# RWKV chunk recurrence in one transformer kernel: the second head pair's turns and first inverse products in the TensorE array's other two quarters

## The chip, the cores and the metric

The kernel runs on one core of a Trainium2 chip. The metric is the device time of one execution, in microseconds (us), the median of several runs.

## The reference

Two small blocks of two layers each, batch 1, 256 tokens, width 1024, all in fp32. The first block has a short convolution mixer, an MLP, an RWKV-7 mixer and an MLP; the second has a top-k sparse attention, an MLP, a forgetting attention and an MLP. The change lies in the RWKV-7 mixer, whose core is this recurrence for each of 16 heads of size 64 (`_wkv7_scan`, shortened):

```python
def frame_step(state, inp):                 # r, w, k, v, a, b of one token
    sa = einsum('bhvk,bhk->bhv', state, a_t)
    state = state * w_t + sa[..., None] * b_t + v_t[..., None] * k_t
    y_t = einsum('bhvk,bhk->bhv', state, r_t)
```

Here a = -kk (the normed key) and b = kk * ah. The result is normed by head, gets a bonus term, is gated and goes through `w_o`.

## The kernel before

The recurrence is computed in chunks of 64 tokens, four chunks. Within a chunk the token-by-token feedback through `sa` becomes a unit triangular 64x64 matrix that has to be inverted. The 16 heads are 8 pairs: in a pair, head 0 lies on partitions 0 to 63 and head 1 on 64 to 127 (`HEAD`). A *slot* is two pairs (`q` or `m` = 0, 1), so there are four slots, and a fifth round for what trails behind.

TensorE works on a pair by `by_head` (line 2562): one 64x64 product for each head, with the operands and the output on the same partitions. Head 0 uses the quarter of the array with rows 0 to 63 and columns 0 to 63, head 1 the quarter with rows and columns 64 to 127. The other two quarters, rows of one head and columns of the other, are not used.

`wkv_steps(slot)` gives the order of steps, and every engine walks through the same list. For slot s they are:

- `gram`, for each pair: the gram products of b and of k with a and r (64x128, into `acc[q]` and `acc[2+q]`), and between them the turn of v from feature-major to token-major (a product with a centred identity, into the second half of bank `un[q]`). VectorE makes from `acc[q]` the first inverse `inv_t`, the masked `nb_t` and the turned inverse `inv_x` (lines 1938 to 1942); ScalarE copies v to `v_tok` (1249).
- `tok`, for each pair: the turns of b and k into `un[q]`; ScalarE copies them to `bk_tok` (1252), and after the second pair makes the exponentials `w_cum`, `w_inv` of the next slot (1124, 1125). VectorE masks `nk_t` (1946).
- five levels j, each doubling the size of the inverted blocks: `t1` for each pair, `n_m` times `inv_x` into `acc[q]`, copied by ScalarE to the tile `t1` (1257); `dx` for each pair, `t1` times `inv_t` into `acc[2+q]`; VectorE adds it to `inv_t` (1951) and turns the result to `inv_x` (1954). `n_m` is masked by POOL (806).
- between these, the *chain* of the slot before, `rhs`, `u` and `sy` for each of four chunks: right-hand side, solution, and state and y. ScalarE copies `wkv_rhs` (1260) and `wkv_u` (1263), VectorE keeps and updates `state` (1963, 1969, 1971) and copies y (1929).

The order in slots 1 to 3, with the pair in brackets: gram(0), rhs, gram(1), u, tok(0), sy, tok(1); then level 1 as t1(0), rhs, t1(1), dx(0), u, dx(1); level 2 as t1(0), sy, t1(1), dx(0), rhs, dx(1); level 3 with u and sy, level 4 with rhs and u, level 5 with sy behind t1(0) alone. In slot 0 there is no chain; there `beside_steps` lays the last value products of the mixer (`value_rows`, full-array products) between the steps. In slots 1 and 2 ScalarE and VectorE also split one half of a weight tile after step 1 and after step 14 (`w_hi`, line 869, and `w_lo`, line 1460). In slots 2 and 3 there are statistics products of the group norm (2538, 2547) and a chain of three VectorE scale instructions before level 4's dx (1919, 1921, 1924). Each engine runs its own instructions in order and waits on semaphores; a step that is late holds all behind it on that engine.

Of the kernel before, what the change touches and what calls it, by code (L numbers as in the profile page):

```python
# [8 lines left out]
ACT = mybir.ActivationFunctionType  # L9
# [14 lines left out]
SLOTS = PAIRS // 2  # L24
CHUNK = 64
CHUNKS = SEQ // CHUNK
# [74 lines left out]
def build(nc, A, out):  # L101

    with ExitStack() as ctx:
        sems = {}

        def sem(name):
            if name not in sems:
                sems[name] = ctx.enter_context(nc.semaphore(name))
            return sems[name]
# [61 lines left out]
        eye, eye_centered = c_("eye"), c_("eye_centered")  # L171
# [35 lines left out]
        rw_r, rw_k, rw_v, rw_c, rw_a, rw_kk = RW  # L207
# [40 lines left out]
        v_tok, inv_t, bk_tok = [], [], []  # L248
# [356 lines left out]
        def half_bank(b, at_):  # L605
            return flat(b)[:, 2 * P * at_:2 * P * (at_ + 1)].rearrange("p (c q) -> p c q", c=CHUNKS)
# [11 lines left out]
        def _(sp):  # L618
# [82 lines left out]
        g_done, gk_done, tok_done, tok_out, inv_ready, lak_ready, end_ready = (  # L701
            sem(n) for n in ("g_done", "gk_done", "tok_done", "tok_out", "inv_ready", "lak_ready", "end_ready"))
# [16 lines left out]
        def _(pool):  # L719
# [25 lines left out]
            def build_bk(s):  # L745
                pool.wait_ge(sem("rw_ready"), s + 1)
                pool.wait_ge(sem("exp_ready"), 2 * s + 2)
                pool.wait_ge(tok_done, 2 * s)
                t = slice(2 * s, 2 * s + 2)
                G.tensor_tensor(b_fm[:].rearrange("p q c s -> p (q c s)"), rw_a[:, t, :].rearrange("p q s -> p (q s)"),  # L750
                                w_inv[:].rearrange("p q s -> p (q s)"), ALU.mult)
                G.tensor_tensor(k_fm[:].rearrange("p q c s -> p (q c s)"), rw_k[:, t, :].rearrange("p q s -> p (q s)"),
                                w_inv[:].rearrange("p q s -> p (q s)"), ALU.mult)
# [99 lines left out]
        def _(act):  # L853
# [390 lines left out]
            for slot in range(SLOTS + 1):  # L1244
                for n, (step, s, j, q) in enumerate(wkv_steps(slot)):
                    if step == "gram":
                        act.wait_ge(g_done, 2 * s + q + 1)
                        act.wait_ge(lo_made, 2 * (BESIDE_SLOT[0] + 1))
                        A_(v_tok[SLOT_SET[s]][:, q, :, :], half_bank(un[q], 1), ACT.Copy).then_inc(tok_out, 1)
                    elif step == "tok":  # L1250
                        act.wait_ge(tok_done, 2 * s + q + 1)
                        A_(bk_tok[SLOT_SET[s]][:, q, :, :, :].rearrange("p b c s -> p (b c s)"), flat(un[q]), ACT.Copy).then_inc(tok_out, 1)
                        if q == 1 and s + 1 < SLOTS:
                            wkv_build(s + 1)
                    elif step == "t1":
                        act.wait_ge(t1_done, 10 * s + 2 * (j - 1) + q + 1)
                        A_(t1[:, q, :, :], half_bank(acc[q], 0), ACT.Copy).then_inc(t1_out, 1)
                    elif step == "rhs":
                        act.wait_ge(rhs_done, CHUNKS * s + j + 1)
                        A_(wkv_rhs[:], two_pairs(stat_ps), ACT.Copy).then_inc(rhs_out, 1)  # L1260
                    elif step == "u":
                        act.wait_ge(u_done, CHUNKS * s + j + 1)
                        A_(wkv_u[:], two_pairs(stat_ps, P), ACT.Copy).then_inc(u_out, 1)
                    beside_steps(slot, n)
                    for group in GROUP_ACT.get(slot, {}).get(n, ()):
                        group_step(*group)
# [903 lines left out]
        def _(pe):  # L2170
# [400 lines left out]
            for slot in range(SLOTS + 1):  # L2571
                for n, (step, s, j, q) in enumerate(wkv_steps(slot)):
# [3 lines left out]
                    if step == "gram":  # L2576
                        if q == 0:
                            pe.wait_ge(built, s + 1)
                            pe.wait_ge(const_mid_in, 16)
                        pe.wait_ge(inv_ready, 12 * s)  # L2580
                        pe.wait_ge(tok_out, 4 * s)
                        if s == SLOTS - 1:
                            pe.wait_ge(scaled, s - 2)
                            pe.wait_ge(bonus_ready, s - 2)
                        for c in range(CHUNKS):
                            ins = by_head(bank4(acc[q])[:, c, :], b_fm[:, q, c, :], ar[r_][:, q, c, :])
                        v = rw_v[:, 2 * s + q, :].rearrange("p (c s) -> p c s", c=CHUNKS)
                        for c in range(CHUNKS):
                            ins = by_head(half_bank(un[q], 1)[:, c, :], v[:, c, :], eye_centered)
                        ins.then_inc(g_done, 1)  # L2590
                        for c in range(CHUNKS):
                            ins = by_head(bank4(acc[2 + q])[:, c, :], k_fm[:, q, c, :], ar[r_][:, q, c, :])
                        ins.then_inc(gk_done, 1)
                    elif step == "tok":

                        pe.wait_ge(tok_out, 4 * s + q + 1)
                        for m, src in ((0, b_fm), (1, k_fm)):
                            for c in range(CHUNKS):
                                ins = by_head(half_bank(un[q], m)[:, c, :], src[:, q, c, :], eye)
                        ins.then_inc(tok_done, 1)  # L2600
                    elif step == "t1":
                        pe.wait_ge(inv_ready, 12 * s + 2 * (j - 1) + q + 1)
                        if j > 1:
                            pe.wait_ge(nm_ready, 8 * s + 2 * (j - 2) + q + 1)
                        for c in range(CHUNKS):
# [325 lines left out]
```

## Time and profile before

| | |
|---|---|
| median of 3 runs | 1378.17 us (1378.03 to 1378.25) |
| profiled execution | 1376.15 us, its span 1374.4 us |
| TensorE busy | 1315.8 us (96%) |
| TensorE weight loads busy | 1143.0 us (83%) |
| VectorE busy | 947.6 us (69%) |
| ScalarE busy | 695.4 us (51%) |
| POOL busy | 119.1 us (9%) |
| slots 0 to 3 of the recurrence | 427.26 to 541.39 us of the span |

An engine's busy time is the union of its instructions' times. TensorE has two rows, PE for the products and PEld for weight loads, which overlap. An fp32 product appears as two records of each. Matmul ends are modelled, so the time from start to start is more exact than a length. In a timeline row the columns are the start in us from the span's start, the length, the engine, the line, the operation, output and inputs, shapes and the number of instructions merged; in brackets the idle time ahead and what ended it.

### The profile page before, as it was taken

How to read it: one execution, taken by the hardware profiler on the slowest of the kernel's cores; microseconds unless marked ns; L12 is line 12 of the kernel's file. 1: busy time of each engine (PE TensorE's matmuls, PEld its weight loads, DVE VectorE, ACT ScalarE, POOL GpSimd, SP SyncE). 2: the span in 40 equal slices, each digit the busy share in tenths (PEclk: the TensorE clock that was granted, in tenths of full speed). 3: DMA queues.
4: the chain of work that ended last, by engine and by line, in shares of the span. 5: the costliest groups of instructions: out<-in, count | busy, mean ns of one | idle time of the engine just before them, and what ended most of it. 6: DMA issues, size and time to landing. Idle time of an engine off the chain costs nothing.

```text
span 1374.4 us, 24879 instructions
## 1 busy us (share of the span) xinstructions
PE 1315.8 (96%) x10501; PEld 1143.0 (83%) x10501; DVE 947.6 (69%) x1419; ACT 695.4 (51%) x1185; POOL 119.1 (9%) x113
## 2 busy tenths in 40 slices
PE   4999999999999999999999997999999999999997
PEld 2998888997999888778888885788888898888886
DVE  1887798976678666675566887666556777766655
ACT  2544644444567344464444647555445667654443
POOL 0000000010100754100000040000000021000000
PEclk9999999999999999999999999999999999999999
DMA  9996899985241012256665532265655544465561
GB/s 360 373 369 235 299 355 380 358 313 179 93 154 32 3 34 92 68 186 200 196 185 175 175 124 93 87 201 181 206 184 184 157 124 153 148 205 184 184 189 57
DMA packets 177559, 256.90 MB, mean 187 GB/s; under 512 B 10472, under 2 KB 122536, under 8 KB 177448
## 3 DMA queue, kind: packets, MB, share of 16 engines
q1 hardware_dynamic: 177448, 255.31, 55.8%
q8 instruction: 83, 1.36, 0.4%
q14 instruction: 28, 0.23, 0.0%
HBM read 254.25 MB, written 1.05 MB: 186 GB/s over the span
## 4 chain that ended last, share of the span: by engine, by line
PE 86%; DVE 8%; ACT 2%; DMA 1%; issue 1%; SPq 1%; DVEq 0%; ACTq 0%
PE acc L2232 11%; PE acc L2234 10%; PE acc L2233 10%; PE un L2175 8%; PE un L2176 7%; PE un L2177 7%; PE side L2213 7%; PE un L2213 6%; PE acc L2562 3%; PE side L2216 3%; PE un L2216 3%; DVE w_lo L1460 2%; DMA stage<-in_conv_w_in 1%; PE side L2562 1%; PE un L2562 1%
## 5 line engine op out<-in xcount | busy, mean ns | idle before, releaser
L1460 DVE TENSOR_TENSOR w_lo<-stage,w_hi 128x1024 fp32r<-128x1024 f32 (+1 forms) x374 | 450.0, 1239 | 157.8 <-ACT w_hi L869 156.9
L869 ACT ACTIVATE w_hi<-stage 128x1024 fp32r<-128x1024 f32 (+1 forms) x378 | 380.1, 1049 | 213.2 <-PE acc L2234 193.1
L2232 PE MATMUL acc<-w_hi,z_hi 128*128 128x512 f32 x640 | 253.0, 395 | 1.7 <-DVE z_lo L1907 1.3
L2234 PE MATMUL acc<-w_hi,z_lo 128*128 128x512 f32 x640 | 249.6, 390 | 0.0
L2233 PE MATMUL acc<-w_lo,z_hi 128*128 128x512 f32 x640 | 249.5, 390 | 0.0
L2175 PE MATMUL un<-h_both,w_hi 128*128 128x256 f32 x736 | 215.3, 292 | 2.7 <-DVE h_both L1518 2.2
L2176 PE MATMUL un<-h_both,w_hi 128*128 128x256 f32 x736 | 208.8, 284 | 0.0
L2177 PE MATMUL un<-h_both,w_lo 128*128 128x256 f32 x736 | 208.6, 283 | 0.0
L2175 PEld LDWEIGHTS un<-h_both,w_hi 128*128 128x128 f32 x736 | 141.5, 192 | 9.9 <-issue 4.9
L2232 PEld LDWEIGHTS acc<-w_hi,z_hi 128*128 128x128 f32 x640 | 120.4, 188 | 28.4 <-issue 3.5
L2176 PEld LDWEIGHTS un<-h_both,w_hi 128*128 128x128 f32 x736 | 141.7, 193 | 1.2 <-issue 0.7
L2177 PEld LDWEIGHTS un<-h_both,w_lo 128*128 128x128 f32 x736 | 141.6, 192 | 0.0
L2234 PEld LDWEIGHTS acc<-w_hi,z_lo 128*128 128x128 f32 x640 | 120.3, 188 | 25.5
L2233 PEld LDWEIGHTS acc<-w_lo,z_hi 128*128 128x128 f32 x640 | 120.5, 188 | 23.6
L2213 PE MATMUL un<-h_both,w_hi 128*128 128x512 f32 x384 | 121.2, 397 | 0.4 <-DVE w_lo L1460 0.4
L2213 PE MATMUL side<-h_both,w_hi 128*128 128x512 f32 x384 | 120.8, 396 | 0.4
L2216 PEld LDWEIGHTS side<-h_both,w_lo 128*128 128x128 f32 x384 | 72.1, 188 | 17.1
L2216 PEld LDWEIGHTS un<-h_both,w_lo 128*128 128x128 f32 x384 | 72.1, 188 | 16.9
L2216 PE MATMUL un<-h_both,w_lo 128*128 128x256 f32 x384 | 75.5, 278 | 0.0
L2216 PE MATMUL side<-h_both,w_lo 128*128 128x256 f32 x384 | 75.4, 278 | 0.0
L1744 DVE SCALAR_TENSOR_TENSOR ada_sum<-ada_buf,small,ada_sum 128x1024 f32<-128x1024 f32 x49 | 62.8, 1282 | 1.4 <-DMA ada_buf<-in_ada_w 0.3
L2213 PEld LDWEIGHTS un<-h_both,w_hi 128*128 128x128 f32 x384 | 59.1, 189 | 1.8 <-DVE w_lo L1460 0.6
(385 smaller groups left out, 1885.0 us busy)
## 6 DMA issues: line engine op xcount, KB each, us to landing
stage<-in_mlp_w SPq DMA_DIRECT2D x64, 1024.0 KB
ada_buf<-in_ada_w SPq DMA_DIRECT2D x48, 1024.0 KB, 11.4
stage<-in_w_up SPq DMA_DIRECT2D x32, 1024.0 KB
stage<-in_w_down SPq DMA_DIRECT2D x32, 1024.0 KB
stage<-in_conv_w_in SPq DMA_DIRECT2D x12, 1024.0 KB
stage<-in_rw_w_rkv SPq DMA_DIRECT2D x12, 1024.0 KB
stage<-in_w_in_a SPq DMA_DIRECT2D x8, 1024.0 KB
stage<-in_w_kv_b SPq DMA_DIRECT2D x8, 1024.0 KB
```

Of the source, the lines that this page charges most:

```text
L869: A_(w_hi[u % 2][:, half, 0:n], stage[u % NSTAGE][:, half, 0:n], ACT.Copy).then_inc(hi_made, 1)
L1460: V.tensor_tensor(w_lo[u % 2][:, half, 0:n], stage[u % NSTAGE][:, half, 0:n], w_hi[u % 2][:, half, 0:n].bitcast(F32), ALU.subtract).then_i ...
L1744: V.scalar_tensor_tensor(out=to[:], in0=rows, scalar=by, in1=to[:], op0=ALU.mult, op1=ALU.add).then_inc(ada_weighed, 1)
L2175: MM(out, hi_l, hi_r, start=start, stop=False, skip_group_check=True)
L2176: MM(out, hi_l, lo_r, start=False, stop=False, skip_group_check=True)
L2177: return MM(out, lo_l, hi_r, start=False, stop=stop, skip_group_check=True)
L2213: MM(pair[:, m, :, :], wh[:, kt, c], h_both[:, kt, :, :], start=(kt == 0), stop=False, skip_group_check=True)
L2216: ins = MM(pair[:, m, 0, :], wl[:, kt, c], h_hi[:, kt, :], start=False, stop=(kt == KT - 1), skip_group_check=True)
L2232: MM(y, z_hi[:, kt, q], wh[:, i, :], start=(first and kt == 0), stop=False, skip_group_check=True)
L2233: MM(y, z_hi[:, kt, q], wl[:, i, :], start=False, stop=False, skip_group_check=True)
L2234: ins = MM(y, z_lo[:, kt, q], wh[:, i, :], start=False, stop=(last and kt == KT - 1), skip_group_check=True)
L2562: ins = MM(out_[rows], lhs[rows], rhs[rows], start=start, stop=stop, skip_group_check=True)
```

## The change

The turns of v, b and k and the products t1 of a slot's second pair (`m == 1`) write *crossed*: head 0, on rows 0 to 63, goes to output partitions 64 to 127, and head 1 to 0 to 63. They so use the two other quarters of the array. Both pairs are issued in one step, interleaved chunk by chunk, so that four 64x64 tiles follow each other. ScalarE undoes the crossing: its copies of the second pair become two instructions of 64 partitions each. The gram products are not crossed, but regrouped: both pairs' b grams and both v turns in `gram(0)`, both pairs' k grams in `gram(1)`; both pairs' b turns in `tok(0)`, both pairs' k turns in `tok(1)`. The v copies wait for both pairs' turns, the bk copies for all four, and t1 of both pairs waits for both inverses and both `n_m`. dx stays as it was, pair by pair.

```diff
@@ GpSimd, build_bk
-                pool.wait_ge(tok_done, 2 * s)
+                pool.wait_ge(tok_done, s)
@@ ScalarE
                     if step == "gram":
-                        act.wait_ge(g_done, 2 * s + q + 1)
+                        act.wait_ge(v_done, s + 1)
                         act.wait_ge(lo_made, 2 * (BESIDE_SLOT[0] + 1))
-                        A_(v_tok[SLOT_SET[s]][:, q, :, :], half_bank(un[q], 1), ACT.Copy).then_inc(tok_out, 1)
+                        if q == 0:
+                            A_(v_tok[SLOT_SET[s]][:, 0, :, :], half_bank(un[0], 1), ACT.Copy).then_inc(tok_out, 1)
+                        else:
+                            for to, rows in zip(HEAD, HEAD[::-1]):
+                                ins = A_(v_tok[SLOT_SET[s]][to, 1, :, :], half_bank(un[1], 1)[rows], ACT.Copy)
+                            ins.then_inc(tok_out, 1)
...
                     elif step == "t1":
                         act.wait_ge(t1_done, 10 * s + 2 * (j - 1) + q + 1)
-                        A_(t1[:, q, :, :], half_bank(acc[q], 0), ACT.Copy).then_inc(t1_out, 1)
+                        if q == 0:
+                            A_(t1[:, 0, :, :], half_bank(acc[0], 0), ACT.Copy).then_inc(t1_out, 1)
+                        else:
+                            for to, rows in zip(HEAD, HEAD[::-1]):
+                                ins = A_(t1[to, 1, :, :], half_bank(acc[1], 0)[rows], ACT.Copy)
+                            ins.then_inc(t1_out, 1)
@@ TensorE
-            def by_head(out_, lhs, rhs, start=True, stop=True):
-
-                for rows in HEAD:
-                    ins = MM(out_[rows], lhs[rows], rhs[rows], start=start, stop=stop, skip_group_check=True)
+            def by_head(out_, lhs, rhs, start=True, stop=True, cross=False):
+
+                for rows, to in zip(HEAD, HEAD[::-1] if cross else HEAD):
+                    ins = MM(out_[to], lhs[rows], rhs[rows], start=start, stop=stop, skip_group_check=True)
                 return ins
...
+                            for m in range(2):
+                                for c in range(CHUNKS):
+                                    ins = by_head(bank4(acc[m])[:, c, :], b_fm[:, m, c, :], ar[r_][:, m, c, :])
+                                ins.then_inc(g_done, 1)
+                            v = rw_v[:, 2 * s:2 * s + 2, :].rearrange("p m (c s) -> p m c s", c=CHUNKS)
+                            for c in range(CHUNKS):
+                                for m in range(2):
+                                    ins = by_head(half_bank(un[m], 1)[:, c, :], v[:, m, c, :], eye_centered, cross=m == 1)
+                            ins.then_inc(v_done, 1)
+                        else:
+                            for m in range(2):
+                                for c in range(CHUNKS):
+                                    ins = by_head(bank4(acc[2 + m])[:, c, :], k_fm[:, m, c, :], ar[r_][:, m, c, :])
+                                ins.then_inc(gk_done, 1)
+                    elif step == "tok":
+
+                        if q == 0:
+                            pe.wait_ge(tok_out, 4 * s + 2)
                         for c in range(CHUNKS):
+                            for m in range(2):
+                                ins = by_head(half_bank(un[m], q)[:, c, :], (b_fm, k_fm)[q][:, m, c, :], eye, cross=m == 1)
+                        if q:
+                            ins.then_inc(tok_done, 1)
+                    elif step == "t1":
+                        if q == 0:
+                            pe.wait_ge(inv_ready, 12 * s + 2 * j)
+                            if j > 1:
+                                pe.wait_ge(nm_ready, 8 * s + 2 * (j - 1))
                             for c in range(CHUNKS):
-                                ins = by_head(half_bank(un[q], m)[:, c, :], src[:, q, c, :], eye)
-                        ins.then_inc(tok_done, 1)
-                    elif step == "t1":
-                        pe.wait_ge(inv_ready, 12 * s + 2 * (j - 1) + q + 1)
-                        if j > 1:
-                            pe.wait_ge(nm_ready, 8 * s + 2 * (j - 2) + q + 1)
-                        for c in range(CHUNKS):
-                            ins = by_head(half_bank(acc[q], 0)[:, c, :], n_m[(j - 1) % 2][:, q, c, :], xn[:, c, :])
-                        ins.then_inc(t1_done, 1)
+                                for m in range(2):
+                                    ins = by_head(half_bank(acc[m], 0)[:, c, :], n_m[(j - 1) % 2][:, m, c, :], inv_x[:, m, c, :], cross=m == 1)
+                            ins.then_inc(t1_done, 2)
```

The copy of `bk_tok` is changed in the same way as those of v and t1, with 512 columns.

## Rows read from the trace of the kernel before

**Rows 1.** Windows of slots 0 to 3: length, busy time of each engine, clock.

```profile
427.26:458.32 31.06, 30.29 (x576) 28.34 (x577) 21.28 (x43) 15.29 (x31) 14.05 (x16) 1.00 0.01 3
458.32:485.71 27.39, 24.17 (x705) 23.00 (x705) 19.49 (x46) 10.51 (x26) 16.02 (x16) 1.00 0.04 9
485.71:513.94 28.23, 26.18 (x712) 24.38 (x713) 20.41 (x50) 13.66 (x32) 19.48 (x19) 1.00 0.10 35
513.94:541.39 27.45, 25.72 (x712) 24.14 (x712) 17.82 (x48) 10.96 (x28) 12.68 (x15) 1.00 0.04 6
```

**Rows 2.** The costliest groups by form, TensorE: busy us, mean ns.

```profile
L2562 PE MATMUL acc<-inv_x,n_m 64*64 64x64 f32 x640 | 25.5, 221 | 3.1 <-DVE inv_x L1954 2.9
```

**Rows 3.** Timeline of TensorE at two places: start, length, records.

```profile
104.19 1.93 PE L2347 MATMUL side<-ada_buf,c_rep 128*32 128x256 f32 x32
...
400.92 1.24 PE L2501 MATMUL acc<-tmp,const 128*128 128x256 f32 x5
```

**Rows 4.** Timeline, second inverse level of slot 0 and the start of the third.

```profile
446.08 1.15 PE L2562 MATMUL acc<-inv_x,n_m 64*64 64x64 f32 x32
446.81 0.85 ACT L1257 ACTIVATE t<-acc 128x256 f32<-128x256 f32 x2 [2.37 <-PE acc L2562]
...
447.24 1.12 PE L2562 MATMUL acc<-inv_t,t 64*64 64x32 f32 x32
447.94 0.29 DVE L1951 TENSOR_TENSOR inv_t<-acc,inv_t 128x128 f32<-128x128 f32 x1 [1.64 <-PE acc L2562]
...
448.93 0.45 DVE L1954 STREAM_TRANSPOSE inv_x<-inv_t 128x256 f32<-128x256 f32 x1
...
449.20 1.15 PE L2562 MATMUL acc<-inv_x,n_m 64*64 64x64 f32 x32
```

**Rows 5.** Timeline, opening of slot 1.

```profile
458.32 1.09 PE L2562 MATMUL acc<-ar,b_fm 64*64 64x128 f32 x16 [0.60 <-DVE inv_t L1951]
...
461.19 1.05 ACT L869 ACTIVATE w_hi<-stage 128x1024 fp32r<-128x1024 f32 x1
...
462.27 1.22 DVE L1460 TENSOR_TENSOR w_lo<-stage,w_hi 128x1024 fp32r<-128x1024 f32 x1
...
465.26 0.45 DVE L1942 STREAM_TRANSPOSE inv_x<-inv_t 128x256 f32<-128x256 f32 x1
...
466.03 0.60 ACT L1252 ACTIVATE bk_tok<-un 128x512 f32<-128x512 f32 x1 [1.04 <-PE un L2562]
...
467.57 0.38 ACT L1257 ACTIVATE t<-acc 128x256 f32<-128x256 f32 x1
...
468.09 0.66 PE L2562 MATMUL acc<-inv_t,t 64*64 64x32 f32 x16 [0.23 <-ACT t L1257]
```

**Rows 6.** Timeline, the five levels of slot 1.

```profile
467.23 0.63 PE L2562 MATMUL acc<-inv_x,n_m 64*64 64x64 f32 x16
...
471.05 0.63 PE L2562 MATMUL acc<-inv_x,n_m 64*64 64x64 f32 x16
...
472.31 1.29 DVE L1460 TENSOR_TENSOR w_lo<-stage,w_hi 128x1024 fp32r<-128x1024 f32 x1
...
475.08 0.63 PE L2562 MATMUL acc<-inv_x,n_m 64*64 64x64 f32 x16
...
476.90 1.99 DVE L1963 TENSOR_SCALAR state_kept<-state,w_end 128x64 f32<-128x64 f32 x2
...
477.57 1.26 POOL L772 TENSOR_TENSOR rw<-rw,rw 128x512 f32<-128x512 f32 x1
...
480.13 0.68 PE L2562 MATMUL acc<-inv_x,n_m 64*64 64x64 f32 x16
...
483.34 0.63 PE L2562 MATMUL acc<-inv_x,n_m 64*64 64x64 f32 x16
```

**Rows 7.** Timeline, slot 2: kept state, and the first of the scale chain.

```profile
499.32 0.40 DVE L1963 TENSOR_SCALAR state_kept<-state,w_end 128x64 f32<-128x64 f32 x2
...
507.57 0.65 DVE L1919 SCALAR_TENSOR_TENSOR rw<-un,rw 128x512 f32<-128x512 f32 x1
```

More of the change, by code:

```diff
@@ L700, in build @@
         cum_ready, exp_ready, built = (sem(n) for n in ("cum_ready", "exp_ready", "built"))
-        g_done, gk_done, tok_done, tok_out, inv_ready, lak_ready, end_ready = (
-            sem(n) for n in ("g_done", "gk_done", "tok_done", "tok_out", "inv_ready", "lak_ready", "end_ready"))
+        g_done, v_done, gk_done, tok_done, tok_out, inv_ready, lak_ready, end_ready = (
+            sem(n) for n in ("g_done", "v_done", "gk_done", "tok_done", "tok_out", "inv_ready", "lak_ready", "end_ready"))
         nm_ready, t1_done, t1_out, dx_done = (sem(n) for n in ("nm_ready", "t1_done", "t1_out", "dx_done"))
@@ L1246, in _ @@
                     if step == "gram":
-                        act.wait_ge(g_done, 2 * s + q + 1)
+                        act.wait_ge(v_done, s + 1)
                         act.wait_ge(lo_made, 2 * (BESIDE_SLOT[0] + 1))
-                        A_(v_tok[SLOT_SET[s]][:, q, :, :], half_bank(un[q], 1), ACT.Copy).then_inc(tok_out, 1)
-                    elif step == "tok":
-                        act.wait_ge(tok_done, 2 * s + q + 1)
-                        A_(bk_tok[SLOT_SET[s]][:, q, :, :, :].rearrange("p b c s -> p (b c s)"), flat(un[q]), ACT.Copy).then_inc(tok_out, 1)
+                        if q == 0:
[4 more added lines that the diff above has]
+                            ins.then_inc(tok_out, 1)
+                    elif step == "tok":
+                        act.wait_ge(tok_done, s + 1)
+                        bk_q = bk_tok[SLOT_SET[s]][:, q, :, :, :].rearrange("p b c s -> p (b c s)")
+                        if q == 0:
+                            A_(bk_q, flat(un[0]), ACT.Copy).then_inc(tok_out, 1)
+                        else:
+                            for to, rows in zip(HEAD, HEAD[::-1]):
+                                ins = A_(bk_q[to], flat(un[1])[rows], ACT.Copy)
+                            ins.then_inc(tok_out, 1)
                         if q == 1 and s + 1 < SLOTS:
@@ L1256, in _ @@
                         act.wait_ge(t1_done, 10 * s + 2 * (j - 1) + q + 1)
-                        A_(t1[:, q, :, :], half_bank(acc[q], 0), ACT.Copy).then_inc(t1_out, 1)
+                        if q == 0:
+                            A_(t1[:, 0, :, :], half_bank(acc[0], 0), ACT.Copy).then_inc(t1_out, 1)
+                        else:
+                            for to, rows in zip(HEAD, HEAD[::-1]):
+                                ins = A_(t1[to, 1, :, :], half_bank(acc[1], 0)[rows], ACT.Copy)
+                            ins.then_inc(t1_out, 1)
                     elif step == "rhs":
@@ L2579, in _ @@
                             pe.wait_ge(const_mid_in, 16)
[L2580 to L2584, printed above, removed]
-                        for c in range(CHUNKS):
-                            ins = by_head(bank4(acc[q])[:, c, :], b_fm[:, q, c, :], ar[r_][:, q, c, :])
-                        v = rw_v[:, 2 * s + q, :].rearrange("p (c s) -> p c s", c=CHUNKS)
@@ L2588, in _ @@
-                        for c in range(CHUNKS):
[L2589 to L2597, printed above, removed]
-                            for c in range(CHUNKS):
-                                ins = by_head(half_bank(un[q], m)[:, c, :], src[:, q, c, :], eye)
-                        ins.then_inc(tok_done, 1)
-                    elif step == "t1":
-                        pe.wait_ge(inv_ready, 12 * s + 2 * (j - 1) + q + 1)
-                        if j > 1:
-                            pe.wait_ge(nm_ready, 8 * s + 2 * (j - 2) + q + 1)
-                        for c in range(CHUNKS):
-                            ins = by_head(half_bank(acc[q], 0)[:, c, :], n_m[(j - 1) % 2][:, q, c, :], xn[:, c, :])
-                        ins.then_inc(t1_done, 1)
@@ new lines, in _ @@
+                            pe.wait_ge(inv_ready, 12 * s)
+                            pe.wait_ge(tok_out, 4 * s)
+                            if s == SLOTS - 1:
+                                pe.wait_ge(scaled, s - 2)
+                                pe.wait_ge(bonus_ready, s - 2)
+                            for m in range(2):
+                                for c in range(CHUNKS):
+                                    ins = by_head(bank4(acc[m])[:, c, :], b_fm[:, m, c, :], ar[r_][:, m, c, :])
+                                ins.then_inc(g_done, 1)
@@ new lines, in _ @@
+                            v = rw_v[:, 2 * s:2 * s + 2, :].rearrange("p m (c s) -> p m c s", c=CHUNKS)
[3 more added lines that the diff above has]
+                            ins.then_inc(v_done, 1)
+                        else:
+                            for m in range(2):
[5 more added lines that the diff above has]
+                            pe.wait_ge(tok_out, 4 * s + 2)
+                        for c in range(CHUNKS):
+                            for m in range(2):
[3 more added lines that the diff above has]
+                    elif step == "t1":
+                        if q == 0:
+                            pe.wait_ge(inv_ready, 12 * s + 2 * j)
+                            if j > 1:
+                                pe.wait_ge(nm_ready, 8 * s + 2 * (j - 1))
+                            for c in range(CHUNKS):
+                                for m in range(2):
+                                    ins = by_head(half_bank(acc[m], 0)[:, c, :], n_m[(j - 1) % 2][:, m, c, :], inv_x[:, m, c, :], cross=m == 1)
+                            ins.then_inc(t1_done, 2)
```

## The prediction

> **What bounds the kernel now.** I read the windows of the stretch that the change touches first. The reader is to see in [rows 1] that slots 0 to 3 take 31.06, 27.39, 28.23 and 27.45 us, that TensorE works in 24 to 30 of each, and that its clock is the full one, so that no clock effect is in play. TensorE at 88 to 97% looks like the bound, and a change that takes TensorE work out looks like a gain of that work. The timelines say otherwise for slots 1 to 3. There one inverse level is a ring: product t1 (TensorE), copy of t1 (ScalarE), product dx (TensorE), add and transpose (VectorE), next t1. Two pairs run round it half a turn apart and the chain steps rhs, u, sy of the slot before fill the gaps. So the reader has to ask of every microsecond taken from TensorE whether the ring gets shorter. In slot 0 the filler is the value product, which can always run, and there TensorE is the bound.
>
> **The unit.** 32 records (four chunks, two heads, two records for each fp32 product, two pairs) take 1.15 us from first start to last end, and one record alone takes 0.22 [rows 2, 4]: 0.93 us for 16 rounds of two records in two quarters, 58 ns a round. The 64x32 products dx take as long (1.12, [rows 4]). One pair's turn, t1 or dx is 0.47 us; in the chain u is 0.23, rhs 0.23 (first chunk) or 0.70, sy 0.70 (first) or 0.93.
>
> **Do four quarters run at once?** No row shows four 64x64 tiles. The nearest: 32 records of four 32-column tiles, all on the same 128 rows, take 1.93 us, 0.24 for four, while full-array records of the same 256 columns take 1.24/5 = 0.25 each [rows 3]. So tiles that share rows and differ in columns overlap fully, and [rows 4] show that tiles which differ in both do. Lower end of the cost of both pairs together: 0.47 us; upper end, no overlap: 0.93. I take 0.47. The Trainium skill, TensorE: Matmul & The Clock Gate, Part 3, says that a weight load overlaps running matmuls only where the row groups differ. By that rule a crossed tile, which shares its rows with a straight one, would wait, and both pairs would take 0.93 as now; the tiles of [rows 3] share all their rows and do not show it.
>
> **What is removed.** TensorE loses 0.47 us per slot in the v turns, 0.93 in the b and k turns and 5 x 0.47 in t1: 3.7 per slot, 15 us in all. That is the gross sum.
>
> **What is added.** (1) The second pair's copies of v, bk and t1 become two instructions on 64 partitions each. A copy of half the partitions and all the columns costs a full one, since its length goes by columns; back to back the 256-column copies start 0.26 apart (the second copy of 0.38 that ends 0.85 after the first starts could be later, as it waits for its product, so 0.47 is the upper end) and the 512-column ones 0.51 (three steps between 466.03 and 467.57, [rows 5]). (2) t1 now waits for the inverses of *both* pairs, so the half turn between them is gone. (3) The chain step that stood between the two t1 now stands between t1 and dx.
>
> **Slot 0.** v turns and b, k turns: TensorE-bound, gain 0.47 + 0.93 = 1.40 to the first t1. VectorE's mixer inputs, which hold the first add until they end, cap it at about 0.98 by the second t1. Each level then: t1 at 0; copy at 0.73; dx of pair 0 at 0.73 + 0.38 + 0.05 = 1.16; its add 0.70 later, 1.86; the second pair's transpose ends 448.93 + 0.45 - 447.94 = 1.44 after that, 3.30; next t1 at 3.35 [rows 4]. The second copies (start 0.26 and 0.52 after the first) are ready at 1.63 and dx of pair 1 at 1.68, hidden behind the VectorE work of pair 0. Before, the level took 449.20 - 446.08 = 3.12, because t1 of pair 0 needed only its own inverse. Three levels lose 0.23 each, the last one (2.9 to the next gram either way) nothing. Slot 0: -0.98 + 0.7 = **-0.3 us**.
>
> **Slot 1**, in us from its first gram product (458.32). G0, G1 0.88 each, v turns 0.47, so rhs of chunk 0 ends at 2.47 as before. Behind it stands the weight half: w_hi at 2.87 and w_lo at 3.95 [rows 5] do not move, so VectorE's second gram block and its transpose end at 465.26 + 0.45 = 7.39 as before. First t1: 7.45, for both (before 7.48 for pair 0, 8.91 for pair 1, [rows 6]). The k turns end at 6.2, their first copy starts at 6.4, the others at 6.9 and 7.4, then the two exponentials, so ScalarE gets to t1 at 8.95 (before 9.25), dx at 9.45 (before 9.77, [rows 5]). A gain of 0.3, and here it stops. Second pair: dx at 10.15, but VectorE reaches its add after the kept y at 11.0 and ends at 11.77: second t1 at 11.8, both (before 12.73 for pair 1). sy 0.93; dx at 13.2 as before; w_hi 12.8 to 13.85, w_lo on VectorE to 15.1 [rows 6], adds at 15.1 and 15.8: third t1 at 16.6 (before pair 1 at 16.76). u; dx at 17.7; sy; dx of pair 1 at 19.1. On VectorE the kept state starts at 19.1. Before, it started at 18.58 and took 1.99 for two multiplies that take 0.40 together undisturbed [rows 7], because POOL's n_m and then L772 held it until 20.5 [rows 6]. POOL's work is not earlier, so the state is again written at 20.6, the second add is at 21.0: fourth t1 at 21.75 (before pair 1 at 21.81). So far level. But before, rhs of chunk 3 stood *ahead* of pair 1's t1; now it comes behind: dx at 21.75 + 0.47 + 0.70 = 22.9, before 21.81 + 0.5 = 22.3; u, dx at 23.7, its transpose ends at 25.25: fifth t1 at 25.3 (before pair 1 at 25.02). sy 0.70, two dx, last at 27.0, add 27.7 to 28.0, next gram at 28.15 against 27.39. Slot 1: **+0.75**.
>
> **Slots 2 and 3** the same way. Slot 2 has the bonus product behind the first dx of level 1 and the variance product behind the first dx of level 2, the same before and after. t1 at 7.4, 12.8, 18.0, 22.7; then the scale chain of VectorE, three instructions from 0.65 us up [rows 7], 21.86 to 23.9 before and 22.6 to 24.6 now, since the fourth level ends later; t1 at 26.3; end 29.1 against 28.23: **+0.9**. Slot 3 has no weight half, so its first t1 comes at 6.1, but ScalarE's copies hold its copy until 7.8: dx 0.75 earlier than before. The bonus product, the state behind POOL and the rhs behind t1 take that back: t1 at 11.8, 17.0, 21.85, 25.45, end 28.15 against 27.45: **+0.7**.
>
> Sum: -0.3 + 0.75 + 0.9 + 0.7 = **+2.0 us**. Behind slot 3 nothing is edited, and TensorE fills its window, so it is carried to the end. The profiled execution took 1376.15 us (span 1374.4) and would take 1378.2; the median of the three runs, 1378.17, lies 2.0 above it, so I say **1380.2**. That is +0.15%, inside the 0.2% (2.8 us) that a measurement of this kernel can tell from no change.
>
> **Rivals.**
> *A. Tiles that share rows take turns.* For: no row with four quarters. Against: [rows 3]. Then every t1 stays 0.93, on the ring, in 20 levels: 9.3; slot 0's front gain goes, 1.0; with the 2.0 above, +12.3: 1390.5. It decides from a round of four at 116 ns. Chance 0.10. Half of it (a round near 85 ns): 1386, 0.08.
> *B. The faster one: VectorE's kept state no longer meets POOL.* The wait of up to 1.6 in level 3 [rows 6] sits on the ring in slots 1 to 3, and if the new order places the two multiplies in a gap of POOL it is gone: 1.2 to 1.6 per slot, -3.6 to -4.8 against +2.0. If the weight half of slots 1 and 2 is passed as well (0.7 each) it is -4.2: 1374. It decides when the kept state starts over 0.2 before POOL's next instruction. For: in [rows 6] a few tenths decide. Against: POOL is busy without a gap there in slot 1. Chance 0.20, half of it under -2.8.
> *C. TensorE-bound after all:* all 15 us come: 1363. Against: ScalarE's copy in [rows 5] and VectorE's add in [rows 6] end the waits. I give it 0.01, in B's.
>
> **Chances and range.** Forecast 0.62 with its own range 1377.5 to 1383: of that 0.02 falls under -0.2%, 0.22 over +0.2%. With B 0.09 below and 0.11 within, A 0.18 above: faster 0.11, same 0.49, slower 0.40. The range leaves out the faster part of B and the full A: 1375.4 to 1387.
>
> **What would show it.** Both pairs' t1 as 32 records in some 0.68 us from start to last end (0.47 + 0.22); if 1.15, A. Two short ScalarE copies, starts 0.26 apart, behind each copy of pair 0. In slot 0 levels of 3.35. In slots 1 to 3 TensorE's busy time down by 3 us or more while the windows grow by half a microsecond to one, with idle time ahead of t1 ended by VectorE's transpose. Kept state still near 1.5 us in slot 1. The prediction is wrong if a slot of 1 to 3 is shorter than now by over 0.3, or if rounds of four take over 65 ns.

## The result, and the profile after

The changed kernel takes 1396.6 us (median of six runs, 1391.4 to 1402.3) against 1378.3 (six runs, 1378.0 to 1380.8): the ratio is 1.0132, 95% interval 1.0117 to 1.0147. It is slower by 18.4 us, where +2 was forecast and 1387 was the upper end of the range. The six times follow the mean granted clock of the run: 1391.4 at 0.990, 1396.9 at 0.982, 1402.3 at 0.978. The profiled execution is the slowest of them, with a span of 1400.5 us, so it shows the loss at its largest.

First the same windows as [rows 1], slots 0 to 3. The columns are the stretch, its length, busy time of TensorE's products and weight loads, VectorE, ScalarE and POOL, the granted clock, DMA share and GB/s.

```profile
428.19:466.16 37.97, 33.41 (x577) 30.80 (x577) 22.57 (x43) 18.32 (x38) 14.73 (x16) 0.76 0.01 2
466.16:500.28 34.12, 26.10 (x704) 24.79 (x705) 18.02 (x46) 13.54 (x33) 15.01 (x16) 0.81 0.03 5
500.28:530.86 30.58, 23.27 (x712) 20.99 (x713) 19.95 (x50) 16.87 (x39) 18.83 (x19) 1.00 0.10 35
530.86:562.38 31.52, 25.30 (x713) 23.61 (x713) 17.80 (x48) 13.99 (x35) 13.93 (x15) 0.87 0.04 5
```

The reader is to see two things. The clock column of [rows 1] held 1.00 four times; now three slots lie between 0.76 and 0.87. And slot 2, at the full clock, is longer too: 30.58 for 28.23. The four slots grew by 20.1 of the 26.1 us between the two spans. Of the other 6.0, 0.9 lie ahead of slot 0, where nothing is edited, and 5.1 behind slot 3; they were not followed up.

The next three windows lie in stretches of the changed kernel with the lower of TensorE's two levels, 1.2 for 2.4 GHz. The first stretch runs from 448.1 to 472.0, through the second half of slot 0 and into slot 1; the last one, from 553.9, ends at 567.6, 5.2 us behind slot 3.

```profile
449.00:455.00 6.00, 5.50 (x92) 5.02 (x92) 1.80 (x6) 1.34 (x4) 4.80 (x7) 0.50 0.01 3
478.80:485.60 6.80, 5.94 (x126) 5.80 (x127) 2.77 (x10) 3.05 (x7) 4.63 (x6) 0.50 0.01 2
553.90:567.50 13.60, 12.34 (x197) 10.91 (x193) 4.20 (x13) 4.94 (x13) 5.79 (x5) 0.50 0.45 146
```

What did TensorE do before the first fall? The window just ahead of it, and the matching one of the kernel before under it:

```profile
443.00:447.00 4.00, 2.32 (x46) 1.92 (x38) 3.90 (x7) 1.14 (x3) 2.11 (x2) 1.00 0.02 4
```

```profile
442.00:446.00 4.00, 3.89 (x78) 3.55 (x77) 2.69 (x7) 0.77 (x2) 1.41 (x2) 1.00 0.02 4
```

TensorE was busy for 2.32 of 4 us where it had been busy for 3.89. The timeline of the changed kernel there, TensorE's part and then VectorE's and POOL's, says what it waited for:

```profile
442.41 0.69 PE L2578 MATMUL acc<-inv_x,n_m 64*64 64x64 f32 x32
443.70 1.45 PE L2578 MATMUL acc<-inv_t,t 64*64 64x32 f32 x32 [0.59 <-ACT t L1269]
...
447.26 0.69 PE L2578 MATMUL acc<-inv_x,n_m 64*64 64x64 f32 x32 [1.21 <-DVE inv_x L1970]
```

```profile
443.64 1.10 DVE L1856 SCALAR_TENSOR_TENSOR rw<-ka_mix,rw 128x512 f32<-128x512 f32 x1
444.66 1.21 DVE L1857 SCALAR_TENSOR_TENSOR rw<-rw,rw 128x512 f32<-128x512 f32 x1
445.80 0.28 DVE L1967 TENSOR_TENSOR inv_t<-acc,inv_t 128x128 f32<-128x128 f32 x1
446.11 0.45 DVE L1970 STREAM_TRANSPOSE inv_x<-inv_t 128x256 f32<-128x256 f32 x1
446.48 0.25 DVE L1967 TENSOR_TENSOR inv_t<-acc,inv_t 128x128 f32<-128x128 f32 x1
446.76 0.45 DVE L1970 STREAM_TRANSPOSE inv_x<-inv_t 128x256 f32<-128x256 f32 x1
```

```profile
443.22 2.11 POOL L806 TENSOR_TENSOR n_m<-nb_t,const 128x256 f32<-128x256 f32 x2 [8.46 <-PE acc L2578]
```

The first row is 32 records, four quarters, in 0.69 us; [rows 4] have 1.15 for the same products. So the quarters do run at once, as taken. But the second t1 starts 19.07 us after the slot's first gram, where it started 18.82 after it before: both pairs wait for the last transpose, at 446.76. And the earlier first t1 let POOL's n_m start at 443.22, beside VectorE's last mixer inputs, which took 1.10 and 1.21 us. In the kernel before they took 0.69 and 0.68, and POOL's n_m (1.41 us) started as they ended.

The slot at the full clock, slot 2, is read on ScalarE:

```profile
507.05 0.60 ACT L1259 ACTIVATE bk_tok<-un 128x512 f32<-128x512 f32 x1 [1.68 <-PE un L2578]
507.67 1.19 ACT L1262 ACTIVATE bk_tok<-un 64x512 f32<-64x512 f32 x2
508.89 0.63 ACT L1124 ACTIVATE w_cum<-rw 128x512 f32<-128x512 f32 x1
509.43 0.61 ACT L1125 ACTIVATE w_inv<-rw 128x512 f32<-128x512 f32 x1
509.95 0.36 ACT L1269 ACTIVATE t<-acc 128x256 f32<-128x256 f32 x1
510.21 0.27 ACT L1276 ACTIVATE wkv_rhs<-side 128x128 f32<-128x128 f32 x1
510.50 0.77 ACT L1272 ACTIVATE t<-acc 64x256 f32<-64x256 f32 x2
```

Whole instructions start before the one ahead has ended (w_inv 0.54 after w_cum, which lasts 0.63). The 64-partition ones do not: the two of bk start 0.62 after a copy of 0.60 and last 1.19 together, and w_cum starts only 1.22 after them. The copy of t1 waits behind them until 509.95, 2.10 after its product started at 507.85.

### The profile page after: what moved, and what is told of

Same layout as the page of the kernel before. It is cut to its first block, busy times and chain, and to the rows that moved or that the text cites. A ratio compares the mean times of both kernels' runs of the same rounds, so it can differ in the third digit from the quotient of the medians.

```text
span 1400.5 us, 24886 instructions
## 1 busy us (share of the span) xinstructions
PE 1323.6 (95%) x10501; PEld 1147.1 (82%) x10501; DVE 946.7 (68%) x1419; ACT 707.2 (50%) x1213; POOL 117.5 (8%) x113
## 4 chain that ended last, share of the span: by engine, by line
PE 86%; DVE 8%; ACT 3%; issue 2%; DMA 1%; SPq 0%; DVEq 0%; ACTq 0%
PE acc L2248 10%; PE acc L2250 10%; PE acc L2249 10%; PE un L2191 8%; PE un L2192 7%; PE un L2193 7%; PE side L2229 6%; PE un L2229 6%; PE acc L2578 3%; PE side L2232 3%; PE un L2232 3%; DVE w_lo L1476 2%; PE side L2578 2%; PE side L2363 1%; PE side L2729 1%
```

## The experiments

All are timed beside the kernel before on the same chip. Ratios are to the kernel before with their 95% interval. The edits are shown shortened, lines left out marked by dots. Windows and timelines are of each kernel's one profiled execution, and the clock can fall at another place in another execution.

### Which part of the change, and which property of t1

**Turns alone.** t1's product and copies are those of the kernel before; the turns of v, b and k are as in the change.

```diff
-    pe.wait_ge(inv_ready, 12 * s + 2 * j)
...
-    for m in range(2):
-        ins = by_head(half_bank(acc[m], 0)[:, c, :], n_m[(j - 1) % 2][:, m, c, :], inv_x[:, m, c, :], cross=m == 1)
...
+    pe.wait_ge(inv_ready, 12 * s + 2 * (j - 1) + q + 1)
...
+    ins = by_head(half_bank(acc[q], 0)[:, c, :], n_m[(j - 1) % 2][:, q, c, :], xn[:, c, :])
```

> Only the turns of v, b and k are crossed and joint; t1 is issued and copied as in the kernel before. Theory (the loss comes from t1: its joint wait and what TensorE no longer has to do around it): 1377 to 1382 us, clock 0.99 or more as in the kernel before, slots 1 to 3 within 0.5 of 27.4, 28.2 and 27.5. Rival 1 (any use of the other two quarters lowers the granted clock): 1385 us or more with clock 0.5 stretches in the recurrence. Rival 2 (the half copies of ScalarE are the loss): two thirds of its extra copies are at t1, so a third of the 18 us is here: 1384.

1379.1 us, 1.0005 (0.9996 to 1.0013): not to be told from no change. Slots at the full clock: 30.85, 27.77, 28.65, 27.08. The loss is not in the turns, and crossing the turns does not lower the clock. The first t1 of slot 0 comes 1.38 us earlier here too (14.22 after the first gram, before 15.60), but the second only 0.40 (18.42 for 18.82): again VectorE's last two mixer inputs take 1.10 and 1.22 beside POOL's n_m. With t1 alone, where the first t1 is not earlier, they take 0.69 and 0.68.

**t1 alone.** The reverse: turns as before, t1 and its copies as in the change.

> Only t1 is crossed and joint; the turns are those of the kernel before. Theory: most of the loss is here, 1388 to 1397 us, with stretches at half the clock from slot 0 on. Rival 2 (half copies, shared by turns and t1): 1390. Rival 3 (the regrouped grams and turns are the loss): 1380.

1389.4 us, 1.0088 (1.0073 to 1.0104): more than half of the loss. Its slot 0 keeps the clock at 1.00 and takes 33.00. One level of it in the timeline:

```profile
445.90 0.70 PE L2567 MATMUL acc<-inv_x,n_m 64*64 64x64 f32 x32
446.67 0.38 ACT L1258 ACTIVATE t<-acc 128x256 f32<-128x256 f32 x1 [2.42 <-PE acc L2567]
...
447.07 0.77 ACT L1261 ACTIVATE t<-acc 64x256 f32<-64x256 f32 x2
...
447.10 1.45 PE L2567 MATMUL acc<-inv_t,t 64*64 64x32 f32 x32 [0.50 <-ACT t L1258]
447.81 0.29 DVE L1956 TENSOR_TENSOR inv_t<-acc,inv_t 128x128 f32<-128x128 f32 x1 [1.96 <-PE acc L2567]
...
448.92 0.45 DVE L1959 STREAM_TRANSPOSE inv_x<-inv_t 128x256 f32<-128x256 f32 x1
...
449.42 0.39 PE L2567 MATMUL acc<-inv_x,n_m 64*64 64x64 f32 x10
```

From one t1 to the next it is 3.52 us: dx 1.20 after t1, the first add 0.71 after dx, the last transpose ends 1.56 after that. The halves start 0.40 behind the whole copy and last 0.77 together, so they end 1.94 after t1. TensorE's weight load for the second pair's dx waits for them until 447.89. The loss of this run is not all ring either: its slot 1 takes 35.59 at a clock of 0.71.

**t1 joint, straight.** Both pairs' t1 behind both inverses in one step, but on their own quarters and with one whole copy each.

```diff
-    pe.wait_ge(inv_ready, 12 * s + 2 * (j - 1) + q + 1)
+    if q == 0:
+        pe.wait_ge(inv_ready, 12 * s + 2 * j)
...
+        for m in range(2):
+            ins = by_head(half_bank(acc[m], 0)[:, c, :], n_m[(j - 1) % 2][:, m, c, :], inv_x[:, m, c, :])
+        ins.then_inc(t1_done, 2)
```

> Both pairs' t1 in one step behind both inverses, as in the change, but not crossed: straight quarters only, one full copy for each pair, turns as before. It has the joint wait and not the shorter product nor the half copies. Theory (joint wait and idle TensorE): 0.4 to 0.6 us more a level than before in slot 0, about 1 to 2 us a slot in slots 1 to 3, +5 to +8 in all, 1383 to 1387, and some stretches at half the clock, fewer than in t1 alone. Rival 2 (the copies): 1379. Rival 1 (the crossing lowers the clock): clock 0.99 or more and at most +4.

1396.7 us, 1.0128 (1.0113 to 1.0144). I had expected at most 1387. It has no crossed product and no half copy, and loses as much as the whole change. So the joint wait is enough for the loss, and against this run t1 alone, with four quarters and half copies, *gives back* 7 us. Its windows, slots 0 to 3:

```profile
429.65:464.02 34.37, 30.58 (x576) 28.36 (x577) 21.28 (x43) 14.74 (x31) 14.02 (x16) 1.00 0.01 3
464.02:499.05 35.03, 29.17 (x704) 28.32 (x705) 17.89 (x46) 10.17 (x26) 15.97 (x16) 0.81 0.02 4
499.05:532.65 33.60, 27.44 (x712) 25.82 (x713) 20.61 (x50) 13.21 (x32) 19.86 (x19) 0.95 0.09 33
532.65:563.47 30.82, 25.75 (x712) 24.22 (x712) 17.80 (x48) 10.50 (x28) 13.18 (x15) 1.00 0.01 3
```

Slots 0 and 3 lose 3.3 and 3.4 us at the full clock; slot 1 falls to 0.81 with straight quarters only.

**t1 crossed, pair by pair.** The waits of before; pair 1 crossed and copied in halves.

> t1 pair by pair with the waits of the kernel before, but pair 1 is crossed and copied in two halves; turns as before. It has the half copies and the crossing, not the joint wait and no less work on TensorE. Theory: +0.1 to +0.4 us in the levels where the copy of pair 1 is on the ring, +2 to +5 in all, 1380 to 1383, clock 0.99 or more. Rival 1 (crossing lowers the clock): 1390. Rival 2 (the copies are the loss): 1388 or more.

1380.6 us, 1.0015 (1.0006 to 1.0023), clock 0.995 in the profiled run. Slot 0 takes 32.74 for 31.06, its levels 3.45 for 3.12; slots 1 and 2 are within 0.12 of before.

**The whole change without the joint wait of t1.**

> The whole change, except that t1 is issued pair by pair, each behind its own inverse; pair 1 still crossed and copied in halves, turns crossed and joint. Theory (the joint wait of t1 is the loss): the costs of the turns alone (+0.6) and of t1 crossed by pair (+2.1) add up, 1379 to 1383 us, slots about 32.5, 27.9, 28.7, clock 0.99 or more. Rival (the turns and the halves together leave TensorE idle enough, whatever the wait): stretches at half the clock in slots 0 and 1, 1388 or more.

1383.7 us, 1.0035 (1.0023 to 1.0048), above the forecast sum of 1381; its profiled run has a clock of 0.89 in slot 1 and 0.94 in slot 2. Taking the joint wait of t1 out of the change, and with it the step in which both pairs' products overlap, gives back 12.9 of the 18.4 us. The rival is not quite dead: turns and halves together can let the clock fall as well.

### Is the clock a part of the loss?

**Idle products in the gaps.** Full-array products whose result is overwritten, first without care for the size of the gap.

```diff
                         ins.then_inc(dx_done, 1)
+                        if q == 1 and j < WKV_LEVELS[-1] and slot == 0:
+                            for _ in range(4):
+                                MM(flat(acc[0])[:, 0:256], ident, const[0][:, 0:256], start=True, stop=True)
```

> The changed kernel, and in slot 0 behind the second dx of levels 1 to 4 four full-array fp32 products of 256 columns whose result nobody reads (about 1.0 us at the full clock, in a gap of 1.2 us or more). Theory (TensorE idles on the joint wait and the granted clock falls for that): the clock stays 1.00 in slot 0, which takes 33 us and not 38, and the whole 1388 to 1392 us. Rival (the clock falls for what the crossed products draw or for another cause, or the gaps are the whole loss): the clock falls as before, with more work at half the clock, 1396 to 1400.

> As the one above, and in slots 1 to 3 three such products ahead of each t1 of levels 2 to 5 (0.75 us in gaps of 0.87 or more). Theory: the clock is 1.00 in all four slots; what is left over the kernel before is the longer ring alone, 1.9 + 3 x 2.3 = 9: 1385 to 1389. Rival (the loss is the ring alone, the clock only follows): no gain over the changed kernel, 1396 or more.

1396.2 and 1396.6 us, ratios 1.0134 (1.0115 to 1.0153) and 1.0134 (1.0121 to 1.0147): no gain. I had mis-sized them. [rows 3] give 0.25 us a record, but an fp32 product is two records, so four take 2.1 us and not 1.0. This line is one of the groups of three, in slot 1 of the second kernel:

```profile
491.40 1.56 PE L2642 MATMUL acc<-const 128*128 128x256 f32 x6
```

The clock did what the theory said (slot 0 of the first kernel, then slots 1 and 2 of the second, each at 1.00), and the four runs of the second kernel have a mean clock of 0.994 to 0.996, where the six of the changed kernel have 0.978 to 0.990. But the products took the place of the gaps and more:

```profile
427.36:465.75 38.39, 34.49 (x608) 31.19 (x609) 22.57 (x43) 18.34 (x38) 14.74 (x16) 1.00 0.01 2
```

```profile
465.24:496.14 30.90, 27.25 (x729) 23.97 (x729) 17.76 (x46) 13.45 (x33) 15.11 (x16) 1.00 0.03 6
496.14:529.06 32.92, 29.03 (x737) 25.22 (x737) 20.61 (x50) 16.89 (x39) 18.83 (x19) 1.00 0.09 32
```

**Fitted to the gaps.** Two of 256 columns behind level 1's last dx in slot 0, one of 224 between t1 and dx in levels 2 to 5, two of 176 ahead of t1 in slots 1 to 3.

> The changed kernel with idle products cut to the gaps (the first filler runs made slot 0's levels 5.2 us, since one such product of 256 columns takes 0.52 and not 0.25): two of 256 columns behind level 1's second dx in slot 0, one of 224 between t1 and dx in its levels 2 to 5, two of 176 ahead of each t1 in slots 1 to 3. Theory: clock 1.00 in all four slots and the ring alone is left: slots 33, 29.8, 30.6 and 29.5, 1385 to 1388 us with little scatter between runs. Rival (the clock is no part of the loss, or is not due to the gaps): 1394 or more.

1389.0 us, 1.0078 (1.0063 to 1.0093), 7.6 us below the changed kernel with *more* work on TensorE, and 1 us above the forecast 1385 to 1388. The fastest run, 1387.4, has a clock of 0.995.

```profile
427.70:460.59 32.89, 30.66 (x588) 27.06 (x589) 22.60 (x43) 18.34 (x38) 14.75 (x16) 1.00 0.01 3
460.59:492.75 32.16, 27.08 (x720) 24.71 (x721) 18.18 (x46) 13.45 (x33) 15.03 (x16) 0.89 0.03 5
492.75:523.35 30.60, 26.45 (x729) 23.38 (x729) 19.97 (x50) 16.89 (x39) 18.85 (x19) 1.00 0.10 36
523.35:552.54 29.19, 25.80 (x729) 23.11 (x729) 17.73 (x48) 14.01 (x35) 12.91 (x15) 1.00 0.03 5
```

Slot 0 goes from 37.97 to 32.89 and slot 3 from 31.52 to 29.19. Slot 1 still falls once.

**The value product spread.** The same work as in the change: the last value product's rows two to a level, none ahead of the first level.

```diff
-                if n == 3:
-                    value_rows(3, misc, range(4))
                 if n in (7, 11, 15, 19):
-                    value_rows(3, misc, range(n // 4 + 3, n // 4 + 4))
+                    value_rows(3, misc, range(n // 2 - 3, n // 2 - 1))
```

> The changed kernel with the last value product's eight rows two to a level in slot 0, none ahead of the first level: the same work, put in the gaps of the levels. Theory: as the filler in slot 0, clock 1.00 there, slot 0 at 33 us or less, 1388 to 1391 in all. Rival: the gap moves ahead of the first t1 and the clock falls there instead: 1394 to 1400.

1392.9 us (1389.1 to 1400.9), 1.0116 (1.0091 to 1.0140): between the two forecasts. Slot 0 takes 35.47 at a clock of 0.95; its levels are 4.20 with two rows each, longer than the 3.52 of a level with one. But slot 1 keeps its clock here:

```profile
465.79:495.57 29.78, 21.49 (x705) 19.74 (x705) 18.03 (x46) 13.45 (x33) 15.09 (x16) 1.00 0.03 6
```

**t1 joint in slot 0 alone, and in slots 1 to 3 alone** (turns as before).

> Kernel before, t1 crossed and joint in slot 0 alone. Theory: slot 0 takes 33.0 as with t1 crossed and joint in all slots, the rest as before: +1.9, 1380 to 1381, clock 0.99 or more. Rival (slot 0 starts the fall of the clock that slot 1 then shows): 1384 or more.

> Kernel before, t1 crossed and joint in slots 1 to 3 alone. Theory: the loss of t1 crossed and joint in all slots less slot 0's 1.9: 1387 to 1388, with stretches at half the clock in slot 1. If the fall of the clock is slot 0's doing: the ring alone, 2.4 + 1.9 + 1.5 = 5.8, 1384. If POOL or the weight halves were the cause in slot 1, its kept state starts as before and the slot is within 0.5 of 27.4.

1382.7 us (1379.2 to 1386.5), 1.0028 (1.0017 to 1.0039), and 1386.8, 1.0059 (1.0047 to 1.0072). In the first, slot 0 takes 33.01 and the unedited slot 1 takes 29.02 at a clock of 0.94 for 27.39: slot 0 hands part of its loss on, so that the run lies over its forecast of 1381. In the second, slot 1 falls without it (31.12 at 0.89). Both happen.

### The half copies

**Halves on their own partitions.** The kernel before, only pair 1's copy of t1 in two instructions, nothing crossed.

```diff
+    for rows in HEAD:
+        ins = A_(t1[rows, 1, :, :], half_bank(acc[1], 0)[rows], ACT.Copy)
```

> The kernel before, with pair 1's copy of t1 as two instructions of 64 partitions each whose input and output lie on the same partitions; nothing crossed. With t1 crossed by pair a level of slot 0 took 3.45 us and not 3.12. If it is the change of partitions between input and output that stops the overlap of ScalarE's instructions: copies 0.26 apart, levels 3.12 to 3.3, 1378.5. If it is two instructions on other partitions than their neighbours: 0.4 apart, 3.45, 1380.5.

1381.2 us, 1.0020 (1.0012 to 1.0029). Levels of 3.51; the timeline of its fourth level in slot 0:

```profile
454.85 0.38 ACT L1258 ACTIVATE t<-acc 128x256 f32<-128x256 f32 x1 [2.27 <-PE acc L2567]
455.32 0.77 ACT L1261 ACTIVATE t<-acc 64x256 f32<-64x256 f32 x2
```

Two copies of 0.38 take 0.77: no overlap, though nothing changes partitions between input and output. So it is not the crossing; why instructions on 64 partitions don't overlap where whole ones do, no run shows.

**Whole copies.** t1 alone crossed and joint, then the whole change, each with pair 1 copied in one instruction. Both kernels leave out bringing pair 1's heads back to their own partitions, so they give prices and not a way to do it.

> t1 crossed and joint as in the run of t1 alone (1389.4), but pair 1's copy is one whole instruction; the heads of pair 1 are not brought back to their own partitions, that part of the computation is left out. If the half copies stand on the ring with the joint wait: 3 to 5 us less, 1385, levels of slot 0 at 3.3. If VectorE's two adds and two transposes hide them, as the levels of 3.52 say (dx of pair 1 ready when its add can start): levels stay 3.5, 1388 to 1390.

> The whole change, with every copy of pair 1 (v, b and k, t1) as one whole instruction; the heads of pair 1 are not brought back. If the half copies of b and k make slot 2's first level long (6.0 us, forecast 5.4): that level is 5.4 or less, slot 2 takes 29.9 and slot 0 about 0.2 less; in all 3 us less than the changed kernel at the same clock. If they are hidden: slot 2 at 30.5.

1388.1 us, 1.0081 (1.0068 to 1.0094), and 1386.9, 1.0064 (1.0049 to 1.0079). At t1 alone the halves cost nothing in slot 2's levels 1 to 3: its second, third and fourth t1 start 13.17, 18.44 and 23.13 us after its first gram, with halves 13.18, 18.45 and 23.13. In slot 0 they do cost, both kernels at the full clock: 33.00 with halves, 32.19 without. A level there:

```profile
446.18 0.69 PE L2562 MATMUL acc<-inv_x,n_m 64*64 64x64 f32 x32 [0.22 <-DVE inv_x L1954]
446.94 0.66 ACT L1257 ACTIVATE t<-acc 128x256 f32<-128x256 f32 x2 [2.88 <-PE acc L2562]
...
447.37 1.12 PE L2562 MATMUL acc<-inv_t,t 64*64 64x32 f32 x32 [0.50 <-ACT t L1257]
448.08 0.29 DVE L1951 TENSOR_TENSOR inv_t<-acc,inv_t 128x128 f32<-128x128 f32 x1 [1.96 <-PE acc L2562]
...
449.06 0.45 DVE L1954 STREAM_TRANSPOSE inv_x<-inv_t 128x256 f32<-128x256 f32 x1
```

The next t1 starts at 449.56, so the level is 3.38 for 3.52, and from the last t1 to the next slot it is 2.91 for 3.24. The first forecast said 3.3 for such a level, the second 3.5; the median fits the second, but slot 1 is at a clock of 0.79 here. In the whole change the median is 9.7 us lower, some of it clock. Slot 2 of the second kernel, for 30.58:

```profile
494.26:523.07 28.81, 22.44 (x713) 20.66 (x713) 19.86 (x50) 13.00 (x32) 18.58 (x19) 1.00 0.11 39
```

Its t1 start 7.57, 12.40, 17.67, 22.36 and 25.94 us after the first gram; with halves 7.57, 13.58, 18.86, 23.55 and 27.39. The first level loses 1.18 of the 1.77, behind the halves of b and k, and the fourth and fifth the rest. Slot 1's last two levels show the same at the full clock: 3.58 and 2.91 with whole copies, 3.84 and 3.25 with halves.

## Why the prediction was wrong

It had two faults of unequal size, in the profiled run 11.7 us, and 6.3 us (8.3 where 2.0 was forecast).

**1. "its clock is the full one, so that no clock effect is in play."** This was read from the rows of before, and it held for the kernel before alone. TensorE was busy there for 24 to 30 us of each slot. The forecast itself took 3.7 us out of each slot, named idle time ahead of t1, and never asked what the granted clock would do with it: the clock is a term that was put at nothing. In the profiled run this costs 5.1 us in slot 0 (37.97 - 32.89), 4.3 in slot 1 (34.12 - 29.78) and 2.3 in slot 3 (31.52 - 29.19), 11.7 together. Over the medians: 18.4 less the ring's 8.3 (below) leaves 10, which can hold more than the clock, as the profiled run lost 6.0 us outside the slots. The filler that holds the clock in three of the four slots brings back 7.6 of it. No rival covered it, and so the range did not reach it; the chance given to a slower kernel stood on the ring's terms and on rival A. The Trainium skill, TensorE: Matmul & The Clock Gate, Part 1, says that the lower clock is the default and that activity lifts it. The rows agree in that: idle products made the kernel faster. They do not show which gap is short enough to be harmless, and the mean clock differs between runs of one kernel (0.978 to 0.990 for the changed one).

**2. The terms of the ring**, at the full clock. Against [rows 1] the slots lose 1.83, 2.39, 2.35 and 1.74 us (32.89, 29.78, 30.58, 29.19), 8.3 in all, where -0.3, +0.75, +0.9 and +0.7 were forecast. The four lengths are of three kernels: slots 0 and 3 with the fitted filler, slot 1 with the value product spread, slot 2 of the changed kernel.

- *Half copies.* "back to back the 256-column copies start 0.26 apart" and "the 512-column ones 0.51": that is the spacing of whole copies. The halves start 0.39 and 0.6 apart, and the instruction ahead and the one behind do not overlap with them either. In slot 2 this is 1.77 of the 2.35. With whole copies the slot loses 0.58, and its t1 start within 0.4 of the forecast 7.4, 12.8, 18.0, 22.7 and 26.3. Slot 1's last two levels, 3.58 and 2.91 with whole copies, were forecast at 3.55 and 2.85. So the walk round the ring was right there and this term of it was mis-sized. In slot 1's first level and in slot 3 the halves were not measured apart at the full clock.
- *Slot 0's gain.* "cap it at about 0.98 by the second t1": it lost 0.25, 1.23 from the forecast. The first t1 did come 1.38 earlier (forecast 1.40), but that moved POOL's n_m onto VectorE's last mixer inputs, 0.94 us longer by it; they also began 0.33 later after the first gram. This was looked for in slots 1 to 3 (rival B), not here.
- *Slot 0's levels.* "next t1 at 3.35": 3.52 at the full clock. This too is the halves. They were to be "ready at 1.63" and "hidden behind the VectorE work of pair 0", and end 1.94 after t1. Adds and transposes then take 1.56 (forecast 1.44). With whole copies these take 1.43 and the level 3.38. The last level was to cost nothing: 2.88 before, 3.24 with halves, 2.91 without. Straight and joint a level takes 3.82, so the joint wait costs 0.70 a level (3.82 - 3.12), the four quarters bring back 0.44 and the halves take 0.14 of that again.

**3. What held.** Four quarters run at once: 0.69 us for a forecast 0.68. Rival A fell. The Trainium skill, TensorE: Matmul & The Clock Gate, Part 3, has a weight load overlap running products only where its row group differs; the measured 0.69 is against that rule for these tiles. TensorE is not the bound in slots 1 to 3: its busy time in slot 2 fell by 2.9 us and the slot grew. The wait goes to VectorE's transpose ahead of t1. Rival B did not come: it made slots 1 to 3 shorter, and slot 1 is longer in every run that has the joint wait there. VectorE's kept state still met POOL in slot 1 at the full clock (1.46 us, forecast near 1.5). The "wrong if" of the forecast (a slot shorter by 0.3, rounds of four over 65 ns) named neither of the two faults; it tested what the change does on TensorE, which was right.

No version here beats the kernel before by what can be measured. The whole change with copies that cost nothing extra would still be at 1386.9, with the clock as it fell there. The turns alone gain 0.2 and 0.4 in slots 0 and 3 and lose 0.4 in each of the others; crossing them in slots 0 and 3 alone was not tried, as 0.6 us could not be told from none. Why slot 1 of the fitted filler still fell, and by what rule a gap is harmless, stays open.

## What to carry to other kernels

Pairing two chains to share a pass joins their waits: each then waits for the later one, and if another engine makes their inputs one after the other, the overlap that hid it is gone. Here that cost 0.70 us a level of slot 0, and the faster product returned 0.44, less 0.14 for its split copies. When a change takes work from TensorE in a stretch where it was nearly always busy, ask what the granted clock will be with the new gaps; a clock of 1.00 before is no answer. And price a split copy as two instructions without overlap to their neighbours, not as two steps of the spacing between whole ones.

## What the runs showed of the hardware

- Half-clock time cost less than half of its length. The slots hold 39.2 us of it (448.1 to 472.0, 478.8 to 485.6, and 553.9 to the end of slot 3 at 562.4), half of which is 19.6, but they lose 11.7. Other engines stood on the ring as well and kept their pace: ScalarE's copy of 128x256 took 0.38 and VectorE's transpose 0.45 at either level.
- Four 64x64 tiles that fill the array take 0.69 us for 32 records; a crossed pair issued behind a straight one 0.98 (t1 crossed, pair by pair), where two straight pairs take 1.15.
- ScalarE instructions on 64 partitions as wide as whole ones take as long (0.38 for 256 columns, 0.60 for 512), and none overlapped with its neighbour; whole ones start 0.26 apart at 256 columns and 0.5 at 512. The Trainium skill, ScalarE: Activation LUTs, What ACT_TABLE_LOAD costs, has instructions back to back overlap by some 93 ns; the whole copies are near it (0.38 long and 0.26 apart, so 0.12), the halves do not overlap.
- VectorE's instructions of 0.69 us took 1.10 and 1.21 beside two POOL multiplies of 128x256, which took 2.11 for 1.41. The turns alone show the same (1.10, 1.22 and 2.15).
